# A router with its small matrix stationary in four column groups, routing in two groups, and the first expert's low parts on one engine

## The reference

```python
x = _layer_norm(ALPHA * x + (1.0 + g1[:, None]) * mix, ln1_g, ln1_b)
u2 = x * (1.0 + sc2[:, None]) + sh2[:, None]
# _hier_moe(u2, ...)
g_logits = un @ w_group + b_group            # 4 groups
e_logits = un @ w_route + b_route            # 16 experts, 4 in each group
g_sel = jnp.argmax(g_logits, axis=-1)        # top-1 group
top_v, top_i = lax.top_k(e_sel, TOP_K)       # top-2 experts in that group
h = jax.nn.silu(un @ w_gate[e]) * (un @ w_up[e]) * comb
y = h @ w_down[e]
```

## Time and profile before

| | us |
|---|---|
| three runs | 1321.33, 1323.35, 1324.0 (median 1323.35) |
| the profiled execution, its own time | 1318.6 |
| its span in the trace | 1316.9 |
| PE busy | 1165.1 (88% of the span) |
| DVE busy | 931.1 (71%) |
| ACT busy | 543.6 (41%) |
| POOL busy | 526.0 (40%) |
| granted clock of TensorE, mean | 0.926 of full |

### The profile page before, as it was taken

The page is one execution under the profiler, slowest core; times in us unless marked ns, Lnnn a source line. Parts: engine busy times, 40 slices in busy tenths (PEclk is TensorE's granted clock), DMA queues, the critical chain, the costliest instruction groups (busy, mean ns, idle before and its releaser), DMA issues. The chain is left out here.

```text
span 1316.9 us, 23159 instructions
## 1 busy us (share of the span) xinstructions
PE 1165.1 (88%) x6515; PEld 947.7 (72%) x6516; DVE 931.1 (71%) x1936; ACT 543.6 (41%) x923; POOL 526.0 (40%) x539
## 2 busy tenths in 40 slices
PE   4789999999998988999996289999999999999457
PEld 0269988998897867888885267787877777788311
DVE  2665988988898796678988976557675666543284
ACT  0354445435444532222221334456555554433253
POOL 1402122202211217665561425455564464444276
PEclk9779999999998989999997589999999999999755
DMA  9704033113302463453444558878998887564475
GB/s 322 282 1 152 18 126 127 64 64 127 127 14 98 139 227 129 144 176 133 140 151 150 185 178 225 226 223 206 268 268 242 228 217 206 136 127 90 98 293 207
DMA packets 106195, 215.15 MB, mean 163 GB/s; under 512 B 18091, under 2 KB 67759, under 8 KB 103187
## 3 DMA queue, kind: packets, MB, share of 16 engines
q1 hardware_dynamic: 85004, 163.14, 35.8%
q0 software_dynamic: 20736, 50.89, 17.3%
q10 hardware_dynamic: 415, 0.63, 0.2%
HBM read 153.93 MB, written 85.96 MB: 182 GB/s over the span
## 5 line engine op out<-in xcount | busy, mean ns | idle before, releaser
L1697 PE MATMUL bank<-parts 128*128 128x256 f32 (+2 forms) x1616 | 568.4, 352 | 35.0 <-DVE parts L1513 19.4
L1699 PE MATMUL bank<-parts 128*128 128x256 f32 (+2 forms) x1616 | 551.9, 342 | 0.0
L1698 PE MATMUL bank<-parts 128*128 128x256 f32 (+2 forms) x1616 | 551.4, 341 | 0.0
L1697 PEld LDWEIGHTS bank<-parts 128*128 128x128 f32 x1616 | 308.2, 191 | 83.1 <-issue 39.6
L1699 PEld LDWEIGHTS bank<-parts 128*128 128x128 f32 x1616 | 307.6, 190 | 35.3
L1698 PEld LDWEIGHTS bank<-parts 128*128 128x128 f32 x1616 | 308.4, 191 | 31.3
L586 POOL TENSOR_TENSOR arena<-arena 128x256 f32<-128x256 f32 (+1 forms) x36 | 26.9, 750 | 302.7 <-DVE h_last L1190 210.2
L1648 PE MATMUL bank<-ident,arena 128*128 128x128 f32 (+3 forms) x792 | 120.1, 285 | 21.5 <-DMA arena<-u_d,tok_now 6.4
L1648 PEld LDWEIGHTS bank<-ident,arena 128*128 128x128 f32 (+3 forms) x792 | 96.1, 148 | 52.2 <-issue 9.9
L944 ACT ACTIVATE arena<-bank,w_now 128x512 f32<-128x512 f32 x96 | 66.2, 689 | 126.2 <-PE bank L1699 73.5
L1506 DVE TENSOR_TENSOR parts<-arena,parts x90 | 104.8, 1220 | 13.4 <-ACT parts L919 13.4
(11 more groups left out here) (286 smaller groups left out, 1580.1 us busy)
## 6 DMA issues: line engine op xcount, KB each, us to landing
arena<-in_w_gate SPq DMA_DIRECT2D x16, 1024.0 KB, 5.8
arena<-in_w_up SPq DMA_DIRECT2D x16, 1024.0 KB, 11.0
arena<-in_w_down SPq DMA_DIRECT2D x16, 1024.0 KB, 13.4
arena<-in_w_ada SPq DMA_DIRECT2D x14, 1024.0 KB, 5.7
ada_arena<-in_w_ada SPq DMA_DIRECT2D x8, 1024.0 KB, 17.8
arena<-in_x_prompt SPq DMA_DIRECT2D x8, 1024.0 KB, 7.0
yT_d<-arena SPq DMA_DIRECT2D x16, 512.0 KB, 5.1
arena<-yT_d SPq DMA_DIRECT2D x16, 512.0 KB, 4.9
```

The costliest lines, as they stand in the source:

```text
L1697: pe.matmul(out, x_hi, w_hi, start=start, stop=False)
L1698: pe.matmul(out, x_hi, w_lo, start=False, stop=False)
L1699: return pe.matmul(out, x_lo, w_hi, start=False, stop=stop)
```

## The change

It has three parts. The router's matrix becomes the stationary operand, padded from 20 to 32 columns; the eight k go to four column groups of the array (rows 32 (k % 4) of bank 6), each group adding two of them, and u2's transpose moves through, 128 columns. This leaves four partial sums with tokens as columns. ACT copies them to memory (`part_evac`), and one more product (`router_sum`) with a 128x20 selection matrix adds the four parts and turns the result back. `router_sum(t - 3)` stands at step k = 5 of the second half of `out_proj(t)`. Second, routing has two groups, tiles 0 to 11 and 11 to 17; the place of the first group's `place_rows` moves. Third, POOL makes no low parts; DVE makes all six of the first expert, four ahead of `x_evac(0)` and two behind `hT_evac(0)`, `weights` goes behind `x_evac(0)`, and the register loads go behind the last two parts. ACT's `u2T_evac(NT - 2)` moves ahead of `norm(NT - 1)`.

```diff
-ROUTE = ((0, 4), (4, 8), (8, 12), (12, 17))
-FIRST_DVE = (2, 4)
+ROUTE = ((0, 11), (11, 17))
+GROUP = max(hi - lo for lo, hi in ROUTE)
...
-        w_rt = at(9216, KD, NR)
-        b_rt = at(9376, NR)
+        w_rt = at(9216, KD, 32)
+        b_rt = at(9472, NR)
+        rt_sel = at(9492, NR)
+        rt_part = at(9512, P)
...
-            def first_lo(n):
-
-                cols = slice(n * SPLIT, (n + 1) * SPLIT)
-                pool.wait_ge(S["w_hi"], n + 1)
-                pool.tensor_tensor(w_lo[:, 0, cols], w_raw[0][:, cols], w_hi[:, 0, cols].bitcast(F32),
-                                   ALU.subtract).then_inc(S["w0_lo"], 1)
-
-            for n in range(FIRST_DVE[0]):
-                first_lo(n)
...
             gather(0, 0)
             gather(1, 1)
-            for n in range(FIRST_DVE[1], E_PARTS):
-                first_lo(n)
...
+            def part_evac(t, n=P):
+                act.wait_ge(S["rt_part_mm"], t + 1)
+                act.activation(rt_part[:, 0:n], bank[6][:, 0:n], ACT.Copy).then_inc(S["rt_part_ok"], 1)
+
...
                     u2T_evac(2 * j + b - 2)
                     split_y(2 * j + b + 2, b, j + 2)
                     norm(2 * j + b, b)
+                    part_evac(2 * j + b - 2)
             u2T_evac(NT - 5)
             split_y(NT - 1, 0, NT // 2 + 1, NS)
             norm(NT - 3, 0)
+            part_evac(NT - 5)
             u2T_evac(NT - 4)
             norm(NT - 2, 1)
+            part_evac(NT - 4)
             u2T_evac(NT - 3)
+            part_evac(NT - 3)
+            u2T_evac(NT - 2)
             norm(NT - 1, 0, NS)
-            u2T_evac(NT - 2)
+            part_evac(NT - 2)
...
+            part_evac(NT - 1, NS)
...
+            dve.wait_ge(S["wout_lo"], OUT_EARLY)
+            o.did(dve.memset(w_rt[:, :, NR:32], 0.0))
+            o.did(dve.tensor_reduce(rt_sel, ident[:].rearrange("p (j r) -> p r j", j=4)[:, 0:NR, :], axis=AX, op=ALU.add))
             dve.wait_ge(S["gate_in"], 16)
...
-                dve.tensor_tensor(logits[0:n, ds(t, 1), :].rearrange("p a r -> p (a r)"), bank[6][0:n, 0:NR], b_rt[0:n, :],
+                dve.tensor_tensor(logits[0:n, ds(t, 1), :].rearrange("p a r -> p (a r)"), bank[6][0:n, 256:256 + NR], b_rt[0:n, :],
...
             ln_out(NT - 2, 1, P, prompt_rows, NT // 2, False)
+            place_rows(*ROUTE[-2])
             dve.wait_ge(S["tiles_s_in"], 16 * 3 * DEC_B)
...
             router_out(NT - 2)
-            place_rows(*ROUTE[-2])
             router_out(NT - 1, NS)
...
+            for n in range(GU_PARTS):
+                first_lo(n)
+            dve.wait_ge(S["idx_ready"], 2)
+            x_evac(0)
             weights()
-            for n in range(*FIRST_DVE):
-                first_lo(n)
-            o.wait()
-            dve.wait_ge(S["w0_lo"], FIRST_DVE[0])
-            dve.memset(spare[0:1, 0:1], 0.0).then_inc(S["w_lo"], GU_PARTS)
-            dve.wait_ge(S["idx_ready"], 2)
-            slots = [next_expert(s) for s in range(3)]
-            x_evac(0)
             hot_weights()
             hidden(0, 0, first=True, weigh=False)
             x_evac(1)
             hT_evac(0)
-            dve.wait_ge(S["w0_lo"], FIRST_DVE[0] + E_PARTS - FIRST_DVE[1])
-            dve.memset(spare[0:1, 0:1], 0.0).then_inc(S["w_lo"], DN_PARTS)
+            for n in range(GU_PARTS, E_PARTS):
+                first_lo(n)
+            slots = [next_expert(s) for s in range(3)]
             slot_rows()
             slot_weights()
...
                     for k in range(KD):
+                        if sums is not None and h == 1 and k == 5:
+
+                            sums()
...
                 for k in range(KD):
-                    last = pe.matmul(bank[6][0:n, 0:NR], u2T[:, k, 0:n], w_rt[:, k, :], start=k == 0, stop=k == KD - 1)
-                last.then_inc(S["rt_mm"], 1)
+                    rows = slice(32 * (k % 4), 32 * (k % 4) + 32)
+                    last = pe.matmul(bank[6][rows, 0:n], w_rt[:, k, :], u2T[:, k, 0:n], start=k < 4, stop=k >= 4)
+                last.then_inc(S["rt_part_mm"], 1)
+
+            def router_sum(t, n=P):
+                pe.wait_ge(S["rt_part_ok"], t + 1)
+                pe.matmul(bank[6][0:n, 256:256 + NR], rt_part[:, 0:n], rt_sel, start=True, stop=True).then_inc(S["rt_mm"], 1)
...
             router(NT - 3)
             turn_u2(NT - 2, 1)
+            router_sum(NT - 3)
             router(NT - 2)
-            ranks(*ROUTE[-2])
+            router_sum(NT - 2)
             turn_u2(NT - 1, 0, NS)
             router(NT - 1, NS)
+            router_sum(NT - 1, NS)
             ranks(*ROUTE[-1])
```

More of the change, by code:

```diff
@@ L204, in build @@
         cum_all = place(ada_arena, 27952, NT + 1, NE)
-        prod_b = place(ada_arena, 28240, 2, 5, NE)
-        f_b = [place(ada_arena, 28400 + n * 20, 5, NGR) for n in range(5)]
+        prod_b = place(ada_arena, 24576, 2, GROUP, NE)
+        f_b = [place(ada_arena, 24960 + n * 48, GROUP, NGR) for n in range(5)]
         gm, m1, m2, off_t = (place(ada_arena, 28500 + n * NT, NT) for n in range(4))
-        mx_b = place(ada_arena, 28568, 5)
-        pos_l = place(ada_arena, 28573, 2, 5)
+        mx_b = place(ada_arena, 25200, GROUP)
+        pos_l = place(ada_arena, 25216, 2, GROUP)
         hot_a = place(ada_arena, 20480, 2 * NT * P // 2).bitcast(BF16).rearrange("p (k t r) -> p k t r", k=2, t=NT)
@@ L280, in build @@
             xres1 mix_ready mix_used var_ready sd_ready z_norm u2_ready x1_ready x1_st0 x1_st1 u2_st0 u2_st1 u2T_mm
-            u2T_ok rt_mm rt_ok m_ready rank_mm rank_used hot_part hot_one w_exp w_expd hot_ready idx_mm idx_ready w_raw0 w_raw1 xg0 xg1 xgT_mm
-            w_hi w_lo w0_lo xT_hi_ok xT_lo_ok gu_mm sil_ok hid_ok hT_mm hT_hi_ok hT_lo_ok dn_mm y_act y_dve ys0 ys1
-            fin_in fin_s_in dump_in g2_in wgt_ok hotw_ready wslot_mm dst_ok yr0 yr1 w_now_ok fvar_ready fsd_ready frs_ready fnorm
+            u2T_ok rt_part_mm rt_part_ok rt_mm rt_ok m_ready rank_mm rank_used hot_part hot_one w_exp w_expd hot_ready idx_mm idx_ready w_raw0 w_raw1 xg0 xg1 xgT_mm
+            w_hi w_lo xT_hi_ok xT_lo_ok gu_mm sil_ok hid_ok hT_mm hT_hi_ok hT_lo_ok dn_mm y_act y_dve ys0 ys1
+            fin_in fin_s_in dump_in g2_in wgt_ok dst_ok yr0 yr1 w_now_ok fvar_ready fsd_ready frs_ready fnorm
             fg_ok fb_ready fb_mm fo_act fo_pool fo_ok fo_stored""".split()}
@@ L1814, in _, with out_proj @@
             mixers(NCH, None, after_slices=2 * NCH)
-            def out_proj(t, b, n=P, first=False, turn_before=None, between=None):
+            def out_proj(t, b, n=P, first=False, turn_before=None, between=None, sums=None):
                 pe.wait_ge(S["yT_lo_ok"], t + 1)
@@ L1888, in _ @@
             out_proj(2, 0, turn_before=lambda: turn_u2(0, 0, first=True))
-            for t in range(3, NT - 1):
-                out_proj(t, t % 2, turn_before=lambda: turn_u2(t - 2, t % 2), between=lambda: route(t))
-            out_proj(NT - 1, 0, NS, turn_before=lambda: turn_u2(NT - 3, 0), between=lambda: route(NT - 1))
+            for t in range(3, NT):
+                out_proj(t, t % 2, P if t < NT - 1 else NS, turn_before=lambda: turn_u2(t - 2, t % 2),
+                         between=lambda: route(t), sums=lambda: router_sum(t - 3))
             router(NT - 3)
             turn_u2(NT - 2, 1)
+            router_sum(NT - 3)
             router(NT - 2)
-            ranks(*ROUTE[-2])
+            router_sum(NT - 2)
             turn_u2(NT - 1, 0, NS)
             router(NT - 1, NS)
+            router_sum(NT - 1, NS)
             ranks(*ROUTE[-1])
@@ L1955, in _ @@
             turn_h(0)
-            pe.wait_ge(S["hotw_ready"], 1)
+            pe.wait_ge(S["hot_ready"], 3)
             for n in range(2 * NT):
@@ L1960, in _ @@
                                  start=n == 0, stop=n == 2 * NT - 1)
-            last.then_inc(S["wslot_mm"], 1)
+            last.then_inc(S["idx_mm"], 1)
             for s in (1, 2):
```

7 lines of the change are left out of this document (4 added, 3 removed).

## The result

The changed kernel takes 1309.36 us (median of 4 runs, 1304.74 to 1310.41), the kernel before beside it 1322.34 (4 runs, 1319.95 to 1324.0): ratio 0.9899, 95% interval 0.9874 to 0.9924. On another chip, later, it was 1311.20 against 1320.68, ratio 0.9924 (0.9896 to 0.9953). The forecast was 1314.0, its range 1308 to 1322. The profiled execution took 1304.74 us, span 1303.0 (before 1316.9).

The account below looks back on a forecast made before the run. PE was taken to bound the output projection, DVE's chain of small operations the path after it. First product -14.3, +4.5 behind it and +0.4 for a slower gather gave -9.4: from 1323.35 to 1314.0 us, range 1308 to 1322.

Parts of the forecast that it names:

- The router, 0.57: PE, each projection tile: eight overlapping products take 0.57 us, the sum 0.30; 0.84 saved of 1.71, period 12.76.
- Rival 1: Router on PE: short products in column groups run one behind another, each tile 0.30 us longer; 1328 us, chance 0.11.
- The two DVE operations, +0.4: Before the first `ln_in`: padding and selection matrix, 0.2 us each on DVE, while PE waits; +0.4 us.
- The loop: Projection up to tile 13: saved routers, two pairs of `ranks` and a DVE wait bring its end from 661.0 to 650.0.
- The choice for eleven tiles: DVE at tiles 13 and 14: 8.1 us in two pieces, each held 3.9 by POOL; `ln_in(15)` at 680.6, 9.6 earlier.
- The last tile, 0: From `ln_in(16)` to the last `router_out`: stays 15.1 us, shorter router paying for copy and sum; bounds -0.5 and +1.0.
- The tables, -2.0: After the last `router_out`: +0.7 us for a sixth tile, -2.7 without POOL's low parts; `idx_ready` 9.0 earlier, at 739.2.
- First product -14.3: Start of the experts' first product: at 747.5, 14.3 us earlier, with DVE's four parts done before x is ready.
- The middle, +4.5: Between first and third expert products: two parts (2.36) and register loads (2.11) on DVE delay `slot_weights`; bounds 0 and 5.
- Rival 2: ACT's copy for `router_sum` comes late, PE waits some 0.5 us per tile, 6 in all; 1320 us, chance 0.16.
- Rival 3: Array drains between whole and grouped products cost PE 0.3 us more per tile, 4 over the loop; 1318 us, chance 0.06.
- Rival 4: Behind the first expert's product, the 4.5 us are hidden because PE has other work ready; 1309.5 us, chance 0.10.

Follow-up runs that it names:

- second execution: The changed kernel, unaltered, run and profiled again on another chip beside the kernel before: 1311.20 us, ratio 0.9924.
- one-group kernel: Changed kernel with all eight router pieces in one column group of 32, one after the other, and the sum over 32 rows: 1329.36 us, ratio 1.0057.
- parts-later kernel: Changed kernel with the first expert's last two low parts and the register loads moved behind the slot weights: 1306.46 us, ratio 0.9903.
- router-only kernel: Kernel before with the router's part of the change alone, old routing groups and old low-part split kept: 1317.05 us, ratio 0.9975.

## Why the prediction was right, and which terms were off

The sum was -9.4 at the third product; behind `ln_in(2)` it is -10.81 (-10.45 in the second execution). By its steps:

- **The router, 0.57:** measured 0.57. The sum was put at 0.30 and takes 0.14; the period came out 12.85, not 12.76. So 0.75 are saved per tile, not 0.84; 1.71 - 0.75 - 0.57 - 0.14 = 0.25 are left over. I put them where the stream changes from one kind of product to another; no run shows that by itself. Rival 1 (groups one after another) is ruled out by the one-group kernel.
- **The two DVE operations, +0.4:** 0. From `h_last` to the first `ln_in` it is 0.92 in both kernels.
- **The loop:** -11.0 at tile 13, measured -9.95 (eleven periods 0.09 too long).
- **The choice for eleven tiles:** `ln_in(15)` 30.6 behind `ln_in(13)`, measured 31.07. The held operations were foreseen as 3.9 for each piece; the second piece has 2.17 and 2.43, some 4.2 above unhindered.
- **`ln_out(15)`, `place_rows`:** 12.2 and 5.2; measured 12.05 and 5.1. `ln_in(16)` -7.0, measured -5.71, the shortfall of the loop carried on.
- **The last tile, 0:** from `ln_in(16)` to the last `router_out` 14.22, not 15.1: -0.9, outside the bound of -0.5. This made up for the loop.
- **The tables, -2.0:** -2.29 from `router_out(16)` on; L1397 and L1399 lost what was foreseen. `idx_ready` -9.0, measured -8.91.
- **First product -14.3:** -14.43.
- **The middle, +4.5:** +3.62, and by other terms. The two parts cost their 2.27, and the table under "The last two parts" shows them: from the first `silu` to ACT's split 8.48 in place of 6.23, in every kernel with this order. The 2.11 for register loads failed as a step. Before, waits (`o.wait()`, POOL's parts) stood between DVE's two parts and the loads; now nothing stands between, and the loads pass beside the parts, here and in the parts-later kernel. That the waits were the cause was not tried by itself. The other 1.38 lie ahead of the parts, where the first `silu` started 8.56 behind the first product's start, 7.18 before, as more of that product ran at the lower clock. This is the profiled execution's, not the change's: the kernel with `ln_in(1)` behind the norm has the same marks up to the first product within 0.2 us, and its `silu` starts 7.21 behind it. So the term is +2.25, and the measured +3.62 lies nearer to the forecast than the term does. What sets the clock's rise in one execution or the other stays open.

The likeliest case was thus the right one, with errors of one sign in the loop (`ln_in(16)` 1.3 short) and of the other behind it (the last tile, the tables, the middle); that they cancel is luck. What the prediction did not say is that the first two parts need each other; it followed the whole change through DVE and PE together, where the single prices tried above did not hold.

Of its signs, the wait of over 4 us ahead of the third product did not come so: PE waits 1.04 there, as before, and 2.35 a little earlier, 3.39 in all.

Rival 2 (copy late) is not in the changed kernel's loop: PE waits for ACT's copy three times, 2.0 us in all and 1.27 at most, and only behind the loop, while DVE is the path. It is real in the router-only kernel, where PE waits 3.3 us for it. The Trainium skill, TensorEngine Tiling (Array Packing), section Performance Considerations, says that after a fourfold speedup copying out of PSUM may become the bottleneck. The router-only trace agrees in so far as PE waits for a copy, but not for the copy's length (0.26); what stood ahead of it on ACT made it late. Rival 3 (drains) had 0.3 per tile beyond the sum; the period is 0.09 beyond it, 1 us over the loop. Rival 4 (the 4.5 hidden, as PE has other work) did not come by its mechanism: PE waited 2.35 longer, and what is missing of the 4.5 are the loads. The first comparison's 1309.36 lies at this rival's 1309.5 all the same; the time could not tell the cases apart, the marks can.

The measured time fell by 13.0 us in the first comparison and 9.5 in the second, the 10.8 and 10.5 of the marks with the toss at the port and the spread of the mixers and experts around them.

## What to carry to other kernels

A stage with two engines near their limits gave nothing, in the marks, to the edit that relieved only one of them: price the parts of a change together, through each engine's stream, and test them singly only to learn how they hang together. Before work is moved into an engine's idle time, look at what ended that idle time: if it was the other engine of a shared port, the moved work waits there too (1.7 us hidden of 5.1), and an idle time that ends with another engine was the better place (3.1 hidden). Register loads and small operations cost nothing here where they passed beside a longer operation or filled a wait, so their place mattered more than their number. Before a mark that comes as forecast is taken for proof, cut its stretch into pieces and see which piece moved: here the clock of one execution made up for a term.

## What was not expected of the hardware

- Two operations that start 0.03 to 0.18 us apart at the port of DVE and POOL decide whether `ln_in(2)` comes 21.4 or about 25 us behind the mixers, one way or the other from execution to execution. With one wait more it came at 21.4 in all three executions profiled; in the time of the runs the gain is not shown.
- Over the 7 us from the start of the experts' first product, the granted clock was between 0.58 and 0.79 from one execution to the other, in kernels in which this product is the same, and the `silu` behind it started between 8.56 and 7.10 us after that start.
- Eight products of 32 stationary columns and 128 moving ones take 0.57 us in four column groups and 1.86 in one; the old form, 128 stationary columns and 20 moving ones, took 1.71.
- DVE's operations are held unequally: beside POOL's x1, L1346 and L1348 stood for 1.19 and 2.21 us, while the reduction L1345 was not held (0.52, as in the changed kernel without POOL beside it).
